# First mixer block of a two-block transformer: stick-breaking heads in two buffers, another order of sums, scores and values, masks in one group, output by row tile

## The chip, the cores and the metric

One NeuronCore of a Trainium2 chip runs the whole kernel. The metric is the time of one execution on the device in microseconds (us), as the median of several runs. TensorE (PE in the profile) multiplies into PSUM, which has eight banks of 512 fp32 columns; VectorE (DVE), ScalarE (ACT) and GpSimd (POOL) work beside it, SyncE (SP) issues the loads of weights. Every engine goes through its own queue in order and waits on semaphores for the others.

## The reference, cut to what matters

Two transformer blocks on 512 tokens of width 1024, all in float32. The change lies in the first block's mixer, where `h` is the normed input times one wide matrix, cut into ten parts:

```
z = (q @ k.T) * scale                         # stick-breaking, 8 heads of 64
log_fail = where(past, log_sigmoid(z) - z, 0)
w = where(past, exp(log_sigmoid(z) + sum of log_fail between), 0)
o_sb = w @ v
log_a = log_sigmoid(g_low @ w_gate_up + b) / 16      # gated linear attention (GLA), 4 heads
o_gla = rms_norm(scan over tokens of decayed k, v, read by q) * silu(g_out)
mix = sigmoid(gate_sb) * (o_sb @ w_proj_sb) + sigmoid(gate_gla) * (o_gla @ w_proj_gla)
x = x + mix @ w_out
```

Then come an MLP of width 4096, a differential attention, an MLP, a short convolution and an MLP, which the change does not touch.

## The kernel before, in words

**Products.** fp32 operands are split into a high and a low part, and a product is three matmuls: high by high, high by low, low by high. Weights are loaded in *quads* of 128x2048 (1 MB) into two slots; ScalarE rounds a quad to `w_hi` (`split_quad`, L1479), VectorE subtracts to `w_lo` (L2017). A slot is free again when TensorE is through with its quad (`quad_done`).

**Woven pieces.** While the attention of the first block runs, the projections that it doesn't need at once (`g_qk`, `g_v`, `gate_sb`, `proj_sb`, `g_out`, `gate_gla`) are woven in: `feed(k)` issues k *pieces*, each 12 matmuls of 512 columns (L881) into one of banks 0 to 3. Four pieces use up one quad. When both quads of a group of four banks are done, VectorE moves each bank out (`move`), and the next group's piece waits for that (`bank_free`).

**A head** of the stick-breaking attention has a chain over all engines. `sb_scores` (L909, with the mask of the diagonal tiles added by a 128x128 matmul, L910) makes the triangle `z` in banks 4 to 6. `sb_soft` on ScalarE takes |z|, exp and log (L1485, L1487, L1489) into the buffer `sb_sp`; VectorE makes the softplus and two tile sums (L2021, L2025, L2027), POOL two more and copies (L569, L572); ScalarE rounds to `sb_hi` (L1499); VectorE subtracts to `sb_lo` (L2031). `sb_sums` (L918, L921) adds the sums of later tokens to `z`; ScalarE takes the exponential twice (L1493, L1494), VectorE subtracts (L2035), `sb_values` (L936) multiplies by the values into bank 7, and VectorE copies a head's output out (L2040). There is one set of the buffers `sb_sp` and `sb_lo`, so `sb_soft` of a head waits for the values of the one before. TensorE's order for head t is written out by hand:

```
for t in range(SB_HEADS):
    if t: feed(4)
    sb_sums(t); feed(2); sb_values(t)
    if t < SB_HEADS - 1: sb_scores(t + 1)
```

The orders of ScalarE, VectorE and POOL are written out in the same way. Before the first head, TensorE turns 31 rows of gains (L960), waits for VectorE to copy them out, and makes the low-rank gate (`gate_low` L946, `gate_up` L956).

**Levels.** GLA is built in eight steps: `level(n)` (L985, 16 matmuls of 128 columns), four pieces behind each of the first seven. POOL makes the differences of the gate sums (`level_diff`, L583, L584), ScalarE their exponentials (`level_exp`, L1516), VectorE the factors (L2134, L2135) and the masked selection (`level_select`, L2142). The first pieces behind level 0 multiply the output of the heads, which ScalarE rounds (L1542) and VectorE subtracts (L2163), 2048 columns each. After the last level the decayed keys (L2198) are turned by TensorE (L1028), then come the states (L991) and the outputs of four row tiles (`gla_out`, L1002, L1004).

**Output of GLA.** Per row tile: VectorE moves it out (L2225), ScalarE squares it (L1576), VectorE and ScalarE make 1/sqrt with a logarithm, an exponential and one Newton step (L1584, L1585, L2230 to L2235), VectorE scales (L2238). TensorE turns the tile (`gla_turn`, L1016), ScalarE writes the high part (L1601), VectorE the low part (L2258), and `multiply_half` (L740) begins `proj_gla`, which goes on at L714.

## Time and profile before

| | |
|---|---|
| median of 3 runs | 2108.38 us (2104.95 to 2108.79) |
| profiled execution: time, span | 2110.67 us, 2108.5 us |
| PE busy | 2023.1 us, 96% of the span |
| DVE, ACT, POOL busy | 1038.4 us (49%), 727.9 us (35%), 144.8 us (7%) |
| granted TensorE clock, mean | 0.986 |
| chain that ended last | PE 83%, DVE 8%, ACT 4%, POOL 2%, issue 2% |
| costliest line | L714 PE, 50% of the chain |

The span is the time from the first to the last instruction of the profiled execution; 2.2 us of its time lie around it. Busy shares are means over stages. The granted clock is the share of full speed at which TensorE may run in a stretch: 1.00 is 2.4 GHz, 0.50 is 1.2 GHz, and values between are stretches with some of both.

### The profile page before, as it was taken

The page shows a single profiled execution, that of the slowest core. Times are in us where ns is not written, and L with a number is a line of the kernel's source. Part 1 is how long each engine was busy: PE and PEld are TensorE (multiplying, and loading weights), DVE is VectorE, ACT ScalarE, POOL GpSimd, SP SyncE. Part 2 cuts the span into 40 slices and gives each one's busy share as a digit, 9 for nine tenths or more (in the row PEclk, how much of TensorE's full clock was granted, in tenths as well). Part 3 has the DMA queues.
Part 4 walks back from the last instruction along what each step waited for, and adds up shares of the span by engine and source line. Part 5 has one row for each costly group of instructions (what it writes and reads, how often), then busy time and mean ns, then how long its engine had stood idle before and what let it go on. Part 6 is the DMA issues. An engine that isn't in the chain of part 4 may idle for free.

```text
span 2108.5 us, 23455 instructions
## 1 busy us (share of the span) xinstructions
PE 2023.1 (96%) x10061; PEld 1702.8 (81%) x10061; DVE 1038.4 (49%) x957; ACT 727.9 (35%) x778; POOL 144.8 (7%) x195
## 2 busy tenths in 40 slices
PE   6998998998999999999999799999999999999998
PEld 5776777877888888888888688888888888888886
DVE  3336457755443334355786653433363646332434
ACT  3343454325232322244455431322331324232222
POOL 1000014000000000011000210000020011000000
PEclk9999999999999999999999999999999999999999
DMA  5311211213232222224222133222323323223231
GB/s 177 100 41 56 64 60 60 80 54 106 90 120 98 86 95 99 100 80 101 65 85 63 60 120 100 87 93 99 100 80 100 100 100 110 88 94 100 99 100 60
DMA packets 98007, 188.44 MB, mean 89 GB/s; under 512 B 3983, under 2 KB 16289, under 8 KB 97921
## 3 DMA queue, kind: packets, MB, share of 16 engines
q1 hardware_dynamic: 93888, 176.17, 25.2%
q0 software_dynamic: 3744, 10.21, 1.8%
q8 instruction: 69, 1.13, 0.2%
q10 hardware_dynamic: 288, 0.79, 0.1%
q14 instruction: 18, 0.14, 0.0%
HBM read 184.01 MB, written 2.10 MB: 88 GB/s over the span
## 4 chain that ended last, share of the span: by engine, by line
PE 83%; DVE 8%; ACT 4%; issue 2%; POOL 2%; DMA 1%; SPq 0%; POOLq 0%; ACTq 0%; DVEq 0%
PE ps L714 50%; PE ps L881 8%; PE ps L726 5%; PE ps L684 4%; PE ps L751 3%; PE ps L1117 2%; PE ps L1123 1%; PE ps L985 1%; PE ps L740 1%; PE ps L1142 1%; PE ps L1071 1%; ACT arena L1639 1%; PE ps L1266 1%; DVE w_lo L1780 1%; DVE w_lo L2017 1%
## 5 line engine op out<-in xcount | busy, mean ns | idle before, releaser
L1780 DVE TENSOR_TENSOR w_lo<-w_raw,w_hi 128x2048 fp32r<-128x2048 f32 x126 | 288.8, 2292 | 714.7 <-ACT w_hi L1318 714.7
L1318 ACT ACTIVATE w_hi<-w_raw 128x2048 fp32r<-128x2048 f32 x126 | 241.5, 1916 | 821.0 <-PE ps L714 684.7
L714 PE MATMUL ps<-a_hi,w_hi 128*128 128x512 f32 x928 | 361.1, 389 | 0.0
L714 PE MATMUL ps<-a_lo,w_hi 128*128 128x512 f32 x928 | 361.1, 389 | 0.0
L714 PE MATMUL ps<-a_hi,w_lo 128*128 128x512 f32 x928 | 361.0, 389 | 0.0
L714 PE MATMUL ps<-w_hi,h_hi 128*128 128x512 f32 x592 | 230.4, 389 | 0.7 <-DVE h_lo L1824 0.7
L714 PE MATMUL ps<-w_hi,h_lo 128*128 128x512 f32 x592 | 230.3, 389 | 0.0
L714 PE MATMUL ps<-w_lo,h_hi 128*128 128x512 f32 x592 | 230.3, 389 | 0.0
L714 PEld LDWEIGHTS ps<-a_hi,w_lo 128*128 128x128 f32 x928 | 174.2, 188 | 36.2
L714 PEld LDWEIGHTS ps<-a_lo,w_hi 128*128 128x128 f32 x928 | 174.2, 188 | 36.1
L714 PEld LDWEIGHTS ps<-a_hi,w_hi 128*128 128x128 f32 x928 | 174.2, 188 | 35.9
L714 PEld LDWEIGHTS ps<-w_hi,h_hi 128*128 128x128 f32 x592 | 111.1, 188 | 24.2 <-issue 1.1
L714 PEld LDWEIGHTS ps<-w_lo,h_hi 128*128 128x128 f32 x592 | 111.1, 188 | 23.1
L714 PEld LDWEIGHTS ps<-w_hi,h_lo 128*128 128x128 f32 x592 | 111.1, 188 | 23.0
L2017 DVE TENSOR_TENSOR w_lo<-w_raw,w_hi 128x2048 fp32r<-128x2048 f32 x36 | 84.0, 2334 | 47.8 <-ACT w_hi L1479 47.7
L535 POOL TENSOR_SCALAR small<-small 128x1 f32<-128x1 f32 x44 | 29.7, 675 | 1125.2 <-ACT qk L1382 1125.2
L1479 ACT ACTIVATE w_hi<-w_raw 128x2048 fp32r<-128x2048 f32 x36 | 68.8, 1912 | 92.1 <-PE ps L881 92.1
L881 PE MATMUL ps<-a_hi,w_hi 128*128 128x512 f32 x192 | 78.6, 410 | 0.0
L881 PE MATMUL ps<-a_lo,w_hi 128*128 128x512 f32 x192 | 76.5, 398 | 0.0
L881 PE MATMUL ps<-a_hi,w_lo 128*128 128x512 f32 x192 | 76.2, 397 | 0.0
L1351 ACT ACTIVATE h_hi<-arena 128x1024 fp32r<-128x1024 f32 x52 | 55.2, 1061 | 53.7 <-DVE arena L1856 40.0
L684 PE MATMUL ps<-w_hi,h_hi 128*128 128x512 f32 x160 | 63.0, 394 | 0.0
(344 smaller groups left out, 3338.0 us busy)
## 6 DMA issues: line engine op xcount, KB each, us to landing
w_raw<-in_w_ff SPq DMA_DIRECT2D x32, 1024.0 KB, 5.1
w_raw<-in_mlp_w_up SPq DMA_DIRECT2D x32, 1024.0 KB, 5.3
w_raw<-in_mlp_w_down SPq DMA_DIRECT2D x32, 1024.0 KB, 5.1
w_raw<-in_w_in SPq DMA_DIRECT2D x26, 1024.0 KB, 5.1
w_raw<-in_attn_w_qkv SPq DMA_DIRECT2D x12, 1024.0 KB, 5.1
w_raw<-in_conv_w_in SPq DMA_DIRECT2D x12, 1024.0 KB, 5.2
w_raw<-in_w_proj_gla SPq DMA_DIRECT2D x4, 1024.0 KB, 5.1
w_raw<-in_w_out SPq DMA_DIRECT2D x4, 1024.0 KB, 5.1
```

The source lines that it names most:

```text
L535: pstep(nc.gpsimd.tensor_scalar(v, sumsq[n % 2][:, i:i + 1], EPS, None, ALU.add))
L684: last = mm(ps[:, bank0 + j], left, right, start=(k == 0 and x == 0), stop=(k == KT - 1 and x == 2))
L714: last = mm(ps[:, bank0 + j], left, right, start=(k == 0 and x == 0), stop=(k == QUAD * quads - 1 and x == 2), skip_group_check=halves)
L726: last = mm(ps[:, bank0 + j], left, right, start=False, stop=(a == QUAD - 1 and x == 2))
L751: last = mm(ps[:, bank0 + j, ts_], left[:, s, a, P * j:P * (j + 1)], right[:, QUAD * qi + a, ts_], start=(half == 0 and qi == 0 and a == 0 ...
L881: last = mm(ps[:, j], left, right, start=(k == 0 and x == 0), stop=(k == QUAD * quads - 1 and x == 2))
L1117: last = mm(ps[:, bank], left[:, k, fs], right[:, k], start=(k == 0 and x == 0), stop=(k == KT - 1 and x == 2))
L1318: nc.scalar.activation(w_hi[:, s], w_raw[:, s], ACT.Copy).then_inc(hi_ready, 1)
L1351: nc.scalar.activation(dst, src, ACT.Copy).then_inc(chunk_hi, 1)
L1479: nc.scalar.activation(w_hi[:, s], w_raw[:, s], ACT.Copy).then_inc(hi_ready, 1)
L1780: tt(w_lo[:, s], w_raw[:, s], w_hi[:, s].bitcast(F32), ALU.subtract).then_inc(lo_ready, 1)
L2017: tt(w_lo[:, s], w_raw[:, s], w_hi[:, s].bitcast(F32), ALU.subtract).then_inc(lo_ready, 1)
```

## The change

It touches the first mixer block alone, in these parts.

- **Start.** The turning of the gains moves ahead, between the two quads of `sb_v`.
- **Heads.** `sb_sp` and `sb_lo` get a second place, in memory of `y_tm`, used by heads 2, 4 and 6; head 0 and the odd heads keep the first. `sb_soft` of a head waits for the values two heads before (head 1 still for those of head 0); the rounding, whose target is shared, still waits for the values one head before. `feed(1)` and the scores of the next head now stand between sums and values.
- **Masks.** The four mask matmuls of a head come after its twelve score matmuls, in one group.
- **Gate.** The log-sigmoid of the gate is one VectorE pass instead of three; its division by 16 goes into the scale of the exponentials. Its scratch lies in `x_tm`.
- **Output of the heads.** Rounded and subtracted in four parts, each with a count of its own; POOL's `level_diff(1)` waits for the last of them.
- **End of the levels.** The decays of keys and queries go ahead of the split of quad 26, on ScalarE and VectorE.
- **Output of GLA.** 1/sqrt is a power on POOL (`refine_gla`), for which ScalarE's squares carry the factor 1/256. `proj_gla` begins with passes that need only the high parts, and the last tiles are turned between the passes. `gla_out(2)` and `gla_out(3)` go one piece earlier. POOL's reload of `x` comes after the four powers.

```diff
@@ -193,7 +193,7 @@
-        u_gate, u_abs, keep = yf[:, 0:2048], yf[:, 2048:4096], yf[:, 2048:4096]
+        u_gate, u_abs, keep = yf[:, 0:2048], xf[:, 0:2048], xf[:, 0:2048]
...
@@ -202,8 +202,12 @@
-        sb_sp, sb_lo, sb_hi = h_hi_f[:, 2048:4096], hhf[:, 2048:4096], hhf[:, 0:2048]
-        sb_t, sb_w, sb_wlo, sb_whi = sb_sp[:, 0:TRI], sb_sp[:, 0:TRI], sb_lo[:, 0:TRI], sb_hi[:, 0:TRI]
+        sb_own = [t % 2 == 1 or t == 0 for t in range(SB_HEADS)]
+        sb_sp = [h_hi_f[:, 2048:4096] if own else yf[:, 2048:4096] for own in sb_own]
+        sb_lo = [hhf[:, 2048:4096] if own else y_r[:, 2048:4096] for own in sb_own]
+        sb_t, sb_w, sb_wlo = ([z_[:, 0:TRI] for z_ in v] for v in (sb_sp, sb_sp, sb_lo))
+        sb_hi = hhf[:, 0:2048]
+        sb_whi = sb_hi[:, 0:TRI]
...
@@ -575,6 +579,8 @@
+                if n == 1:
+                    pool.wait_ge(osb_lo, TT)
...
@@ -591,7 +597,14 @@
+            def refine_gla(c):
+                cs = slice(4 * c, 4 * c + 4)
+                pool.wait_ge(gss_ready, c + 1)
+                pstep(nc.gpsimd.tensor_scalar(gvar[:, cs], gss[:, cs], EPS, None, ALU.add))
+                nc.gpsimd.tensor_tensor(grstd[:, cs], gvar[:, cs], halves, ALU.pow).then_inc(ggs_ready, 1)
+            for c in range(TT):
+                refine_gla(c)
...
@@ -851,7 +864,18 @@
-            gemm("sb_v", A, True)
+            p = ph["sb_v"]
+            for qi in range(2):
+                pe.wait_ge(lo_ready, p.q + qi + 1)
+                if qi == 0:
+                    pe.wait_ge(banks_free, p.b - 1)
+                multiply(hi=a_hi, lo=a_lo, s=slot_of(p, 0, qi), qi=qi, bank0=4 * (p.b % 2), quads=2,
+                         token_major=True).then_inc(quad_done, 1)
+                if qi == 0:
+                    pe.wait_ge(banks_free, p.b)
+                    pe.wait_ge(gains_in, GAIN_LOADS * 16)
+                    nc.tensor.transpose(ps[:, SIDE, 0:N_GAINS], gain_rows[0:N_GAINS],
+                                        ident[0:N_GAINS, 0:N_GAINS]).then_inc(gains_turned, 1)
...
@@ -873,6 +895,8 @@
+                    if name == "proj_sb" and blk == 0 and j == 0:
+                        pe.wait_ge(osb_lo, k + 1)
...
@@ -907,13 +931,14 @@
-                    last = mm(out_[:, 0:P], ident_b[:], strict_b[:], start=False, stop=True, skip_group_check=True)
+                for j in range(TT):
+                    last = mm(z[:, COL[j]:COL[j] + P], ident_b[:], strict_b[:], start=False, stop=True, skip_group_check=True)
...
-                for part in (sb_hi, sb_lo):
+                for part in (sb_hi, sb_lo[t]):
...
@@ -967,10 +990,11 @@
-                feed(2)
-                sb_values(t)
+                feed(1)
...
+                feed(1)
+                sb_values(t)
...
@@ -1037,23 +1061,31 @@
-            feed(2)
+            feed(1)
...
-            feed(3)
+            feed(4)
...
-            for i in range(TT - 1):
-                gla_turn(i)
+            s0, bank0 = slot_of(p, 0, 0), 4 * (p.b % 2)
+            gla_turn(0)
+            gla_turn(1)
...
+            pe.wait_ge(hi_ready, p.q + 1)
+            pe.wait_ge(turned_hi, turn_base["o_gla"] + 4)
+            half_pass(s0, 0, bank0, 0, 0)
+            gla_turn(2)
+            pe.wait_ge(turned_lo, turn_base["o_gla"] + 4)
+            half_pass(s0, 0, bank0, 0, 1)
+            gla_turn(3)
...
-            pe.wait_ge(turned_lo, turn_base["o_gla"] + 4)
-            multiply_half(a_hi, a_lo, slot_of(p, 0, 0), 4 * (p.b % 2), 0, range(0, 2))
-            gla_turn(TT - 1)
-            multiply_half(a_hi, a_lo, slot_of(p, 0, 0), 4 * (p.b % 2), 0, range(2, 4))
+            half_pass(s0, 0, bank0, 0, 2)
+            pe.wait_ge(turned_hi, turn_base["o_gla"] + 8)
+            half_pass(s0, 0, bank0, 1, 0)
...
-            multiply_half(a_hi, a_lo, slot_of(p, 0, 0), 4 * (p.b % 2), 1).then_inc(quad_done, 1)
+            half_pass(s0, 0, bank0, 1, 1)
+            half_pass(s0, 0, bank0, 1, 2).then_inc(quad_done, 1)
...
-            multiply(a_hi, a_lo, slot_of(p, 0, 1), 1, 4 * (p.b % 2), 2, False, True).then_inc(quad_done, 1)
+            multiply(a_hi, a_lo, slot_of(p, 0, 1), 1, bank0, 2, False, True).then_inc(quad_done, 1)
...
@@ -1480,23 +1512,28 @@
             def sb_soft(t):
                 act.wait_ge(z_ready, t + 1)
-                if t:
+                if t and sb_own[t] == sb_own[t - 1]:
                     act.wait_ge(sb_pv, t)
-                nc.scalar.activation(sb_t, z, ACT.Abs).then_inc(sb_abs, 1)
+                elif t:
+                    act.wait_ge(sb_pv, t - 1)
...
@@ -1480,23 +1512,28 @@
-                nc.scalar.activation(sb_hi, sb_sp, ACT.Copy).then_inc(sp_hi, 1)
+                if t:
+                    act.wait_ge(sb_pv, t)
+                nc.scalar.activation(sb_hi, sb_sp[t], ACT.Copy).then_inc(sp_hi, 1)
...
@@ -1522,30 +1559,31 @@
                 act.wait_ge(up_mm, h + 1)
                 nc.scalar.activation(u_gate[:, SEQ * h:SEQ * (h + 1)], ps[:, SIDE], ACT.Identity,
                                      bias=b_gate[:, h:h + 1]).then_inc(u_out, 1)
...
+            for t in range(SB_HEADS):
                 n = 6 + 3 * (t // 2)
...
+                sb_weights(t)
+                if t == SB_HEADS - 1:
+                    break
+                if t % 2 == 0:
+                    split_quad(n + 2)
+                sb_soft(t + 1)
                 if t % 2:
+                    split_quad(n + 4)
+                sb_round(t + 1)
+                if t % 2 == 0:
                     split_quad(n + 3)
...
+                if t == 0:
+                    nc.scalar.activation(u_abs, u_gate, ACT.Abs).then_inc(u_read, 1)
+                    act.wait_ge(u_read, 1)
+                    step(nc.scalar.activation(u_abs, u_abs, ACT.Exp, scale=-1.0))
+                    nc.scalar.activation(u_abs, u_abs, ACT.Ln, bias=1.0).then_inc(gate_log, 1)
+                if t == SB_HEADS - 2:
+                    gate_tiles(gates_sb, 4)
+            level_exp(0)
+            act.wait_ge(osb_out, SB_HEADS)
+            for k in range(TT):
+                nc.scalar.activation(o_hi[:, k], o_sb[:, k], ACT.Copy).then_inc(osb_hi, 1)
+            split_quad(19)
             gate_tiles(gates_sb, 5)
             for n in range(1, 4):
                 level_exp(n)
...
@@ -1560,10 +1598,11 @@
-            split_quad(26)
...
-            nc.scalar.activation(elast, b_cum.rearrange("p (m n) -> p m n", n=P)[:, :, P - 1], ACT.Exp).then_inc(g_exp, 1)
+            nc.scalar.activation(elast, b_cum.rearrange("p (m n) -> p m n", n=P)[:, :, P - 1], ACT.Exp,
+                                 scale=1.0 / GLA_TAU).then_inc(g_exp, 1)
+            split_quad(26)
...
@@ -1601,6 +1625,17 @@
+            gla_squares(0)
+            gla_squares(1)
+            split_quad(28)
+            gla_squares(2)
+            gla_squares(3)
+            gla_high(0)
+            gla_high(1)
+            split_quad(29)
+            gla_high(2)
+            gla_high(3)
...
@@ -2060,12 +2099,9 @@
-            def gate_parts():
-                dve.wait_ge(u_read, 1)
-                step(ts(u_gate, u_gate, 0.0, None, ALU.min))
+            def gate_sum():
...
-                step(tt(u_gate, u_gate, u_abs, ALU.subtract))
-                step(ts(u_gate, u_gate, 1.0 / GLA_TAU, None, ALU.mult))
+                step(stt(u_gate, u_gate, 0.0, u_abs, ALU.min, ALU.subtract))
...
@@ -2074,56 +2110,63 @@
             def gate_scan():
                 nc.vector.tensor_tensor_scan(b_cum, keep, u_gate, 0.0, ALU.mult, ALU.add).then_inc(b_ready, 1)
                 dve.wait_ge(b_ready, 1)
...
+            sb_softplus(0)
+            dve.wait_ge(low_mm, 1)
+            nc.vector.tensor_copy(low_t, ps[0:GLA_RANK, SIDE]).then_inc(low_out, 1)
+            sb_softplus_lo(0)
             for t in range(0, SB_HEADS, 4):
                 n, g = 6 + 3 * (t // 2), 3 * t // 4
...
+                sb_weights_lo(t)
                 split_quad(n + 2)
...
+                sb_softplus(t + 1)
+                sb_out(t)
                 move(g, 0)
                 move(g, 1)
...
+                sb_softplus_lo(t + 1)
                 move(g, 2)
...
                 move(g, 3)
...
                 split_quad(n + 3)
                 sb_weights_lo(t + 1)
+                if t == 0:
+                    gate_sum()
+                sb_softplus(t + 2)
+                sb_out(t + 1)
+                move(g + 1, 0)
                 split_quad(n + 4)
...
+                sb_softplus_lo(t + 2)
+                move(g + 1, 1)
+                move(g + 1, 2)
                 if t == 0:
                     gate_keep()
...
+                move(g + 1, 3)
+                sb_weights_lo(t + 2)
+                split_quad(n + 5)
+                sb_softplus(t + 3)
+                sb_out(t + 2)
+                sb_softplus_lo(t + 3)
+                if t == 0:
                     gate_scan()
...
+                else:
+                    dve.wait_ge(sb_pv, SB_HEADS - 1)
+                    step(nc.vector.memset(g_at, 0.0))
+                split_quad(n + 6)
                 move(g + 2, 0)
                 move(g + 2, 1)
...
+                sb_weights_lo(t + 3)
                 move(g + 2, 2)
...
+                if t + 4 < SB_HEADS:
+                    sb_softplus(t + 4)
+                    sb_out(t + 3)
+                    move(g + 2, 3)
+                    split_quad(n + 7)
+                    sb_softplus_lo(t + 4)
+                else:
+                    move(g + 2, 3)
+                    sb_out(t + 3)
...
             b_chunk = b_cum.rearrange("p (m n) -> p m n", n=P)
...
@@ -2158,9 +2201,10 @@
+            for k in range(TT):
+                dve.wait_ge(osb_hi, k + 1)
+                tt(o_lo[:, k], o_sb[:, k], o_hi[:, k].bitcast(F32), ALU.subtract).then_inc(osb_lo, 1)
...
-            dve.wait_ge(osb_hi, 1)
-            tt(o_lo, o_sb, o_hi.bitcast(F32), ALU.subtract).then_inc(osb_lo, 1)
...
@@ -2193,10 +2237,10 @@
-            split_quad(26)
...
+            split_quad(26)
```

**Order on TensorE around a head's scores.** Before (head 2; ahead of these rows are two pieces and the values' first matmuls):

```order
L936 MATMUL ps<-h_hi,arena_r 128x256 x3
L936 MATMUL ps<-h_hi,arena_r 128x128 x3
L909 MATMUL ps<-qk_r 128x512 [waits w_exp]
L909 MATMUL ps<-qk_r 128x512 x2
L910 MATMUL ps<-strict_b,ident_b 128x128
L909 MATMUL ps<-qk_r 128x384 x3
L910 MATMUL ps<-strict_b,ident_b 128x128
L909 MATMUL ps<-qk_r 128x128 x3
L910 MATMUL ps<-strict_b,ident_b 128x128
L909 MATMUL ps<-qk_r 128x256 x3
L910 MATMUL ps<-strict_b,ident_b 128x128
L881 MATMUL ps<-a_hi,w_hi 128x512 [waits lo_ready]
```

With the change (head 3; pieces, L905, on both sides, the values, L961, one piece later):

```order
L905 MATMUL ps<-w_hi,a_hi 128x512
L905 MATMUL ps<-w_lo,a_hi 128x512
L905 MATMUL ps<-w_hi,a_lo 128x512
L933 MATMUL ps<-qk_r 128x512 [waits w_exp]
L933 MATMUL ps<-qk_r 128x512 x2
L933 MATMUL ps<-qk_r 128x384 x3
L933 MATMUL ps<-qk_r 128x128 x3
L933 MATMUL ps<-qk_r 128x256 x3
L935 MATMUL ps<-strict_b,ident_b 128x128 x4
L905 MATMUL ps<-w_hi,a_hi 128x512 [waits bank_free]
L905 MATMUL ps<-w_lo,a_hi 128x512
L905 MATMUL ps<-w_hi,a_lo 128x512
```

The scores no longer follow the values, pieces stand on both sides of them, and the masks come together at their end.

**Order on ScalarE in two heads.** Before (weights of head 3, a split, softplus and rounding of head 4, a split, its weights):

```order
L1493 ACTIVATE h_hi_f<-ps 128x1280 [waits c_ready]
L1494 ACTIVATE h_hi<-ps 128x1280
L1479 ACTIVATE w_hi<-w_raw 128x2048 [waits quad_done,raw_full1]
L1485 ACTIVATE h_hi_f<-ps 128x1280 [waits sb_pv,z_ready]
L1487 ACTIVATE h_hi_f<-h_hi_f 128x1280 [waits sb_abs]
L1489 ACTIVATE h_hi_f<-h_hi_f 128x1280 [waits sb_exp]
L1499 ACTIVATE h_hi<-h_hi_f 128x2048 [waits sp_after,sp_summed]
L1479 ACTIVATE w_hi<-w_raw 128x2048 [waits quad_done,raw_full0]
L1493 ACTIVATE h_hi_f<-ps 128x1280 [waits c_ready]
```

With the change (weights of head 2 in the second buffer, split, softplus and rounding of head 3 in the first, split, its weights):

```order
L1528 ACTIVATE y_tm<-ps 128x1280 [waits c_ready]
L1529 ACTIVATE h_hi<-ps 128x1280
L1511 ACTIVATE w_hi<-w_raw 128x2048 [waits quad_done,raw_full1]
L1520 ACTIVATE h_hi_f<-ps 128x1280 [waits sb_pv,z_ready]
L1522 ACTIVATE h_hi_f<-h_hi_f 128x1280 [waits sb_abs]
L1524 ACTIVATE h_hi_f<-h_hi_f 128x1280 [waits sb_exp]
L1536 ACTIVATE h_hi<-h_hi_f 128x2048 [waits sb_pv,sp_after,sp_summed]
L1511 ACTIVATE w_hi<-w_raw 128x2048 [waits quad_done,raw_full0]
L1528 ACTIVATE h_hi_f<-ps 128x1280 [waits c_ready]
L1529 ACTIVATE h_hi<-ps 128x1280
```

The softplus of the next head still follows the weights, with a split between; its scores come before the values now, and the target alternates between `h_hi_f` and `y_tm`.

**Order on VectorE at the end of the levels.** Before (silu, split of quad 26, decayed keys and queries, last selection):

```order
L2155 TENSOR_TENSOR arena<-arena 128x4x512 [waits gates_made]
L2017 TENSOR_TENSOR w_lo<-w_raw,w_hi 128x2048 [waits hi_ready]
L2198 TENSOR_TENSOR h_lo_f<-h_lo_f,qk 128x2048 [waits g_exp]
L2199 TENSOR_TENSOR h_lo_f<-h_lo_f,h_hi_f 128x2048
L2142 COPY_PREDICATED y_tm<-masks,ps 128x2048 [waits g_sel,g_mm,dve_step]
```

With the change:

```order
L2198 TENSOR_TENSOR arena<-arena 128x4x512 [waits gates_made]
L2241 TENSOR_TENSOR h_lo_f<-h_lo_f,qk 128x2048 [waits g_exp]
L2242 TENSOR_TENSOR h_lo_f<-h_lo_f,h_hi_f 128x2048
L2056 TENSOR_TENSOR w_lo<-w_raw,w_hi 128x2048 [waits hi_ready,dve_step]
L2185 COPY_PREDICATED y_tm<-masks,ps 128x2048 [waits g_sel,g_mm]
```

The split, which waits for TensorE to finish a quad, has moved behind the two decays.

## Rows read from the trace of the kernel before

**Rows 1.** Waits of TensorE up to 500 us: total us, times, longest us.
```profile
PE ps L918 <- DVE h_hi L2031: 6.3, 6, 4.0
PE ps L1016 <- DVE a_lo L2258: 6.0, 1, 6.0
PE ps L881 <- issue: 5.7, 1, 5.7
PE ps L1028 <- DVE y_tm L2142: 3.7, 1, 3.7
PE ps L946 <- DVE gains L2008: 3.2, 1, 3.2
PE ps L936 <- DVE h_hi L2035: 2.2, 1, 2.2
```

**Rows 2.** Stretches (from:to, length, busy us and instructions by engine, PEclk, DMA share, GB/s).
```profile
99.39:105.50 6.11, 6.11 (x14) 4.79 (x15) 2.35 (x4) 2.72 (x2) 1.33 (x4) 0.50 0.34 130
136.30:139.50 3.20, 3.20 (x10) 2.52 (x10) 0.00 (x0) 2.83 (x3) 0.00 (x0) 0.50 0.00 0
176.70:180.00 3.30, 3.29 (x13) 3.00 (x13) 3.30 (x1) 0.00 (x0) 0.00 (x0) 0.58 0.00 0
265.70:269.00 3.30, 3.30 (x11) 2.58 (x11) 0.10 (x1) 3.02 (x3) 0.00 (x0) 0.54 0.86 259
323.70:327.50 3.80, 3.72 (x9) 2.98 (x10) 3.80 (x1) 3.59 (x2) 3.80 (x2) 0.51 0.00 0
436.10:440.00 3.90, 3.82 (x16) 3.50 (x17) 2.54 (x3) 0.00 (x0) 0.00 (x0) 0.57 0.00 0
491.50:495.00 3.50, 3.41 (x17) 3.44 (x18) 2.92 (x8) 1.68 (x4) 0.00 (x0) 0.54 0.77 292
```

**Rows 3.** Stretches: one level with four pieces behind it; the four pieces alone.
```profile
336.47:350.94 14.47, 14.47 (x81) 12.58 (x80) 10.85 (x8) 1.91 (x1) 4.38 (x2) 1.00 0.22 72
339.96:350.94 10.98, 10.98 (x51) 9.10 (x50) 8.87 (x7) 0.00 (x0) 4.38 (x2) 1.00 0.30 96
```

**Rows 4.** Timeline of one head (start us, us, engine, line, out<-in [idle before <-releaser]).
```profile
190.39 0.68 DVE L2040 COPY arena<-ps 64x512 f32<-64x512 f32 x1 [2.21 <-PE ps L936]
...
193.66 1.24 ACT L1485 ACTIVATE h_hi_f<-ps 128x1280 f32<-128x1280 f32 x1 [11.10 <-PE ps L910]
...
197.55 1.49 DVE L2021 SCALAR_TENSOR_TENSOR h_hi_f<-ps,h_hi_f 128x1280 f32<-128x1280 f32 x1 [6.48 <-ACT h_hi_f L1489]
...
200.56 1.92 ACT L1499 ACTIVATE h_hi<-h_hi_f 128x2048 fp32r<-128x2048 f32 x1 [3.04 <-POOL h_hi_f L572]
...
202.51 2.29 DVE L2031 TENSOR_TENSOR h_hi<-h_hi_f,h_hi 128x2048 fp32r<-128x2048 f32 x1 [2.67 <-ACT h_hi L1499]
...
204.85 0.85 PE L918 MATMUL ps<-h_hi,ntri 128*128 128x512 f32 x3 [0.26 <-DVE h_hi L2031]
...
207.08 1.24 ACT L1493 ACTIVATE h_hi_f<-ps 128x1280 f32<-128x1280 f32 x1 [2.80 <-PE ps L921]
```

**Rows 5.** Timeline, TensorE: masks in the scores here and in the later attention.
```profile
191.17 0.23 PE L910 MATMUL ps<-strict_b,ident_b 128*128 128x128 bf16 x1
...
191.33 0.79 PE L909 MATMUL ps<-qk_r 64*128 64x384 f32 x3
...
1029.70 0.40 PE L1178 MATMUL ps<-causal_b,ident_b 128*128 128x128 bf16 x4
```

**Rows 6.** Timeline, ScalarE: the third level exponential.
```profile
331.47 1.92 ACT L1516 ACTIVATE h_hi_f<-h_hi_f 128x2048 f32<-128x2048 f32 x1 [4.10 <-POOL h_hi_f L584]
```

**Rows 7.** Timeline, VectorE, ahead of the transposed keys.
```profile
425.47 2.29 DVE L2017 TENSOR_TENSOR w_lo<-w_raw,w_hi 128x2048 fp32r<-128x2048 f32 x1 [4.15 <-ACT w_hi L1479]
```

**Rows 8.** Timeline, TensorE and ScalarE, where the output is turned.
```profile
483.83 1.80 PE L1016 MATMUL ps<-consts,arena 128*128 128x128 f32 x15
...
486.88 3.01 ACT L1601 ACTIVATE a_hi<-ps,gains 128x256 fp32r<-128x256 f32 x8
```

**Rows 9.** Groups by form, POOL: a small power (busy us, mean ns, idle us).
```profile
L536 POOL TENSOR_TENSOR small<-small 128x1 f32<-128x1 f32 x44 | 39.3, 893 | 3.7
```

141 lines of the change are left out of this document (38 added, 103 removed).

## The prediction

> **What bounds the kernel now.** I read the page first: TensorE is busy for 96% of the span and holds 83% of the chain that ended last. So only what TensorE waits for, what its own instructions take and which clock it is granted can move the time. A busier or idler VectorE costs nothing until TensorE waits for it. The waits of TensorE come next: ahead of 500 us, outside the first 95 us, six groups stand for 27.1 us [rows 1]. The reader is to see that all of them lie in the block that is changed, and that only two are made of several pieces. Third, the table of stretches. After each of the long waits, and twice without one (at 136.3 and 265.7), TensorE runs for 3 to 6 us at half clock or near it [rows 2]. A stretch of length L with granted clock c gives back L x (1 - c): 3.1 + 1.6 + 1.4 + 1.5 + 1.9 + 1.7 + 1.6 = 12.8 us. The block's own work is dense elsewhere: a level with four pieces takes 14.47 us, the four pieces 10.98, one piece 2.74 [rows 3].
>
> **Start.** The turning of the gains moves into `sb_v`, where VectorE waits between two splits, so their copy is over before the scores end. Its 3.2 us of wait (L946) go [rows 1], and with them the 6.1 us at half clock behind it, 3.1 us [rows 2]. Gain 6.3.
>
> **Heads.** From the last mask to the sums, the chain takes 11.2 us: softplus on ScalarE from 193.66, VectorE from 197.55, rounding from 200.56, subtraction 202.51 to 204.80, sums at 204.85 [rows 4]. TensorE has four pieces, 10.98, as cover [rows 3], so a usual head waits only 0.26. In two heads VectorE was late with gate work, and those hold most of the 6.3 of L918 and all the 2.2 of L936 [rows 1]. With the change the scores stand one piece and the values earlier, so five pieces and the values cover the chain: 13.7 us and more against 11.2. The rounding still waits for the values of the head before, and from there only 1.9 + 2.3 lie ahead of the sums. VectorE also has two passes less over the gate. So all 8.5 us go, and the low clock at 136.3, 176.7 and 265.7, 4.5 us. For the two without a wait ahead I note that values and scores stood together just before; a piece now parts them.
>
> Two new waits come in. Head 1 still uses head 0's buffer, so its softplus starts only at the end of values 0. VectorE's queue has that softplus ahead of the output's copy and of bank 0's, which the ninth piece needs: 3.9 + about 2.3 + 0.7 + 0.7 = 7.6 us after the values [rows 4] (the copies from L2040, a like size), against two pieces, 5.5. TensorE waits 2.1. After that, ScalarE has rounding, a split and three passes over the gate to do ahead of head 1's weights: 3.9 + 3.0 + 1.9 + 1.9 + 5.8 and two exponentials of 1.2 are 18.9 us after values 0, where TensorE wants scores 2 after 5.5 + 2.1 + 5.5 + 2.2 + 2.7 = 18.0. Wait 0.9. In all other heads scores wait for those two exponentials, which begin at 207.08 [rows 4] and end 2.4 later, under one piece of 2.74; the margin is 0.3, so I charge nothing. Heads: 8.5 + 4.5 - 3.0 = 10.0.
>
> **Masks.** A mask between scores takes 0.16 from its start to the next start; four in a row in the later attention take 0.40 with the last one's whole length of 0.23, so 0.06 each [rows 5]. Three of the four masks of a head, and perhaps the last, save 0.10: 8 x 0.33 = 2.6 us at most; bounds 0 and 2.6, and I take 2.6, since L1178 is the same instruction with the same kinds of operands.
>
> The Trainium skill ("TensorE: Matmul & The Clock Gate", LDWEIGHTS) puts a load of 128 columns at 128/1.2, some 107 ns, whatever it holds. By it a mask in a group would stay at 0.11, and the masks would give an estimated 1.7. The rows disagree: 0.06 from start to start.
>
> **Output of the heads.** The wait of 5.7 before the first piece of `proj_sb` (L881) [rows 1] is for one rounding and one subtraction of 2048 columns, after each other. In four parts of about 0.5 and 0.6 the last is ready 3.1 us after level 0 began, and level 0 takes 3.5 (14.47 less 10.98) [rows 3]. Wait gone, and 1.9 of low clock at 323.7. But POOL's differences now begin at that end, 3.9 later than before. The third exponential began at 331.47 [rows 6], 17.2 after level 0; now 21.1. Behind it come 1.9, a split 1.9 on ScalarE, 2.3 on VectorE and a selection, which I take at 2.5 for its 2048 columns: 29.7, where level 2 wants to start at 28.9. New wait 0.8. Gain 5.7 + 1.9 - 0.8 = 6.8.
>
> **End of the levels.** VectorE idled 4.15 ahead of the split of quad 26 [rows 7], with the two decays (2.3 each) behind it. Now they lie in that gap, and the last selection ends 4.5 earlier. The 3.7 of L1028 go, and 1.7 of low clock: 5.4.
>
> **Output of GLA.** TensorE turned three tiles only after VectorE's low parts: 6.0, L1016 [rows 1]. Now it needs the high parts of two tiles: turning takes 1.8, ScalarE's eight copies 3.0 from half a microsecond after the start [rows 8], so a wait of 1.8 stays. Then the passes cover the rest: 16 matmuls of 256 columns take 2.0, a turning 0.9, and the ScalarE split between takes 1.9. The powers on POOL take 0.9 for one column [rows 9]; even at twice that they end before VectorE comes to them, and two outputs go a piece earlier. The reload of `x` on POOL's queue starts somewhat later and is not needed before `w_out`. Gain 6.0 - 1.8 = 4.2, and 1.6 of low clock at 491.5 if it doesn't return: 5.8.
>
> **Sum.** 6.3 + 10.0 + 2.6 + 6.8 + 5.4 + 5.8 = 36.9 us. The clock is what I trust least. Waits of 1.8 to 2.2 remain, one of them next to turning. In the trace 2.2 at L936 was followed by no low stretch, but two stretches came with no wait at all. I leave two stretches of 1.6 in place: 33.7. Against the profiled execution's 2110.7 that is 2077.0; it ran 2.3 above the median of 2108.4, so 2074.7 for the median.
>
> The Trainium skill (same page, Part 4) says that transposes don't count as activity for the clock. By it turning and wait together, 1.8 + 1.8, would look idle and the output of GLA would keep its 1.6. That it happens there or elsewhere, the two stretches left in the sum hold it.
>
> **Rivals.**
> *The clock isn't given back* (18%). Waits go, but low stretches stay as long as before at other places; 136.3 and 265.7 speak for it, the missing one after L936 against. 36.9 - 12.8 = 24.1, so 2084.3.
> *VectorE's queue makes the new wait* (10%). What I charge in head 1 alone happens in all seven: softplus ahead of the bank copies. For it: ScalarE's softplus comes behind a split in half of the heads. Against: in the later heads softplus starts with the scores, one piece and the values earlier, which leaves over 2 us. At 2.1 each in six more heads, 12.6 less: 2087.3.
> *Masks cost the same in a group, buffers buy nothing* (7%). The change doesn't do what it says there: a usual head waited 0.26 only, so two buffers alone are worth about 1.3. 33.7 - 2.6 - 1.3: 2078.6.
> *Slower: TensorE at half clock in the heads* (3%). Half-row scores, short sums and values are now scattered between pieces; if each head drew low stretches, each of 3.2 us would cost 1.6. To eat 36.9 us and 4.2 more, it takes 26, over three in each head; from there on the kernel is slower, about 2113. The trace has two in seven heads without a wait.
>
> **How the numbers follow.** My forecast has 62%: 2074.7, its own range 2069 to 2081. The range reaches down to 2067 (all of 36.9, a full set of masks and the lower edge of the runs, 3.4 under the median) and up to 2088, which takes in the first three rivals. A measurement here tells about 0.2%, 4.2 us, from no change. Faster by more: 0.96; within: 0.01; slower: 0.03.
>
> **What would show it.** TensorE's waits up to 475 us under 8 us, and none for the gains, for VectorE's subtraction at the first head-output piece, or at the transposed keys. A wait near 2 in head 1 for VectorE's bank copy, one below 1 ahead of scores 2, one near 1.8 between turning and the first pass. Mask rows of x4 with 0.40. Usual heads closer together by 0.6 (0.26 and the masks' 0.33). It is wrong if sums still wait in later heads, if level 1 or 2 wait more than 1 us for the selection, or if the stretches at half clock add up to more than 6 us of loss in the block.

## The result, and the profile after

The changed kernel takes 2067.66 us (median of four runs, 2065.21 to 2069.64) against 2108.59 for the kernel before (2104.95 to 2108.84): 40.9 us less. The ratio on record is 0.9817, 95% interval 0.9805 to 0.9829; the two medians by themselves give 0.9806. The forecast was 2074.7 with 2067 to 2088, so the time lies in the range, but only 0.7 us above its lower end, and below the forecast's own 2069 to 2081. The profiled execution of the changed kernel took 2065.21 us, its span is 2063.4, its mean granted clock 0.996 (before 0.986).

TensorE's waits up to 500 us in the changed kernel (total, times, longest). They answer to [rows 1]; L784 lies in the work ahead of the block and waited 19.0 before as well.

```profile
PE ps L784 <- DVE y_tm L1920: 19.0, 3, 14.0
PE ps L905 <- DVE h_lo_f L2088: 2.1, 1, 2.1
PE ps L764 <- ACT a_hi L1625: 1.9, 1, 1.9
PE ps L905 <- DVE qk L2096: 1.6, 1, 1.6
PE ps L1009 <- DVE arena L2079: 0.9, 1, 0.9
PE ps L933 <- ACT h_hi L1529: 0.6, 1, 0.6
```

Sums (L943) and values (L961) are gone from the list, and so are the gains and the transposed keys. What the block still waits is 7.1 us, against 28.0 before: 27.1 of [rows 1] and a wait of 0.9 at L985 that was there too and stayed (L1009).

The whole block, from the first scores to the first product of `proj_gla` at full width (busy us and instructions by engine, granted clock, DMA share, GB/s): before, then after with one usual head.

```profile
92.60:506.30 413.70, 385.68 (x1886) 318.97 (x1886) 243.87 (x228) 180.21 (x162) 46.11 (x47) 0.96 0.20 64
```
```profile
92.80:464.90 372.10, 364.97 (x1886) 308.07 (x1886) 235.56 (x207) 177.78 (x157) 53.48 (x55) 1.00 0.22 71
190.00:212.80 22.80, 22.80 (x115) 19.05 (x113) 11.70 (x12) 9.88 (x7) 1.33 (x4) 1.00 0.28 93
```

The block is 41.6 us shorter, and the granted clock in it is 1.00: none of the seven low stretches of [rows 2] is left. Of the 41.6, 20.9 are waits (28.0 less 7.1) and 12.8 the low stretches; that leaves 7.9, and most of it is in scores and masks. These are the rows of head 4's scores in the changed kernel, beside [rows 5]:

```profile
192.88 2.19 PE L933 MATMUL ps<-qk_r 64*128 64x512 f32 x12
195.01 0.40 PE L935 MATMUL ps<-strict_b,ident_b 128*128 128x128 bf16 x4
195.21 0.48 PE L905 MATMUL ps<-w_hi,a_hi 128*128 128x512 f32 x1
```

From the first score to the piece behind the masks it is 195.21 - 192.88 = 2.33 us. Before, the same stretch (of head 3) is this:

```profile
190.28 0.96 PE L909 MATMUL ps<-qk_r 64*128 64x512 f32 x3
...
193.40 0.23 PE L910 MATMUL ps<-strict_b,ident_b 128*128 128x128 bf16 x1
193.44 0.48 PE L881 MATMUL ps<-w_hi,a_hi 128*128 128x512 f32 x1
```

That is 3.16 us. Each of eight heads saves 0.83, 6.6 us in all; I had forecast 0.33 and 2.6. Two usual heads are now 22.79 us apart (scores at 170.09 and 192.88) instead of 24.08 (190.28 and 214.36), 1.29 less: 0.83 for the masks, 0.26 for the wait, and 0.20 that I can't place, which over seven heads is about the rest of the 7.9. The chain of the same head, which answers to [rows 4], now ends in time:

```profile
195.44 1.24 ACT L1520 ACTIVATE y_tm<-ps 128x1280 f32<-128x1280 f32 x1 [2.92 <-PE ps L935]
...
202.31 1.92 ACT L1536 ACTIVATE h_hi<-y_tm 128x2048 fp32r<-128x2048 f32 x1 [1.22 <-POOL y_tm L576]
...
205.17 2.29 DVE L2070 TENSOR_TENSOR y_r<-y_tm,h_hi 128x2048 fp32r<-128x2048 f32 x1
...
210.85 0.73 PE L943 MATMUL ps<-h_hi,ntri 128*128 128x512 f32 x3
```

The subtraction ends at 207.46 and the sums start at 210.85 without a wait, a margin of 3.4 us. The program behind the block, which the change does not touch, is 3.7 us shorter in this execution (from 506.3 and 464.9 to the end). Nearly all of it is the clock. In the kernel before, two waits of TensorE there, of 1.8 and 2.5 us, were each followed by a stretch at half clock, 3.4 us in all:

```profile
979.40:982.80 3.40, 3.40 (x10) 2.62 (x9) 1.74 (x4) 2.03 (x3) 0.00 (x0) 0.50 0.00 0
1136.40:1139.80 3.40, 3.40 (x9) 2.63 (x9) 2.88 (x9) 0.23 (x2) 0.00 (x0) 0.50 0.72 278
```

In the changed kernel the same two waits (1.5 and 2.5) were not. Of the twelve profiles below five have neither stretch. So these come and go from one execution to the next; without them the spans differ by 41.7, near the 40.9 between the medians.

### The profile page after: what moved, and what is told of

Same layout as the page of the kernel before. It is cut to its first block, busy times and chain, and to the rows that moved or that the text cites. A ratio compares the mean times of both kernels' runs of the same rounds, so it can differ in the third digit from the quotient of the medians.

```text
span 2063.4 us, 23442 instructions
## 1 busy us (share of the span) xinstructions
PE 1999.3 (97%) x10061; PEld 1689.5 (82%) x10061; DVE 1030.2 (50%) x938; ACT 726.2 (35%) x773; POOL 152.9 (7%) x203
## 4 chain that ended last, share of the span: by engine, by line
PE 87%; DVE 6%; ACT 3%; POOL 1%; DMA 1%; issue 1%; SPq 0%; POOLq 0%; ACTq 0%; DVEq 0%
PE ps L727 51%; PE ps L905 11%; PE ps L739 5%; PE ps L697 4%; PE ps L764 4%; PE ps L1149 2%; PE ps L1155 1%; PE ps L1009 1%; PE ps L1103 1%; PE ps L933 1%; PE ps L1174 1%; ACT arena L1674 1%; PE ps L1298 1%; DVE w_lo L2056 1%; PE ps L961 1%
## 5 line engine op out<-in xcount | busy, mean ns | idle before, releaser
L905 PE MATMUL ps<-a_hi,w_hi 128*128 128x512 f32 x192 | 77.2, 402 | 2.1 <-DVE h_lo_f L2088 2.1
L905 PE MATMUL ps<-a_hi,w_lo 128*128 128x512 f32 x192 | 74.9, 390 | 0.0
L905 PE MATMUL ps<-a_lo,w_hi 128*128 128x512 f32 x192 | 74.8, 390 | 0.0
```

The source lines that it names most:

```text
L905: last = mm(ps[:, j], left, right, start=(k == 0 and x == 0), stop=(k == QUAD * quads - 1 and x == 2))
```

## The experiments

Twelve kernels. "Against" is the difference of medians to the kernel named; the ratio is to the kernel before, run beside it on the same chip. The median of the kernel before was 2108.59 beside the changed kernel and 2106.01 to 2107.41 beside the others, so a difference to the changed kernel can be off by some 2.6 us. The last column leaves that out: it is the same difference in the profiled executions, for the block alone, from head 0's first score to the first product of `proj_gla` at full width (413.7 us before, 372.1 in the changed kernel).

| | median us | ratio to before (95%) | against | block in the trace |
|---|---|---|---|---|
| masks only | 2098.19 | 0.9958 (0.9945 to 0.9972) | before -9.2 | -8.1 |
| half-row masks | 2098.98 | 0.9963 (0.9951 to 0.9974) | before -8.4 | -8.3 |
| start only | 2100.10 | 0.9966 (0.9954 to 0.9978) | before -7.3 | -7.4 |
| masks apart | 2079.14 | 0.9859 (0.9840 to 0.9878) | changed +11.5 | +12.9 |
| old order, two buffers | 2081.20 | 0.9883 (0.9868 to 0.9898) | changed +13.5 | +14.3 |
| new order, one buffer | 2082.23 | 0.9889 (0.9874 to 0.9905) | changed +14.6 | +15.9 |
| head output whole | 2068.58 | 0.9818 (0.9804 to 0.9831) | changed +0.9 | +1.7 |
| and factor ahead of it | 2073.13 | 0.9843 (0.9829 to 0.9857) | changed +5.5 | +6.6 |
| split 26 first | 2075.01 | 0.9844 (0.9829 to 0.9859) | changed +7.4 | +8.4 |
| low parts first | 2068.56 | 0.9817 (0.9802 to 0.9832) | changed +0.9 | +0.2 |
| waits taken out | 2062.11 | 0.9788 (0.9775 to 0.9802) | changed -5.6 | -5.3 |
| select ahead of split | 2059.55 | 0.9779 (0.9764 to 0.9793) | changed -8.1 | -6.7 |

### What the masks cost

Masks alone, in the kernel before:

```diff
-                    last = mm(out_[:, 0:P], ident_b[:], strict_b[:], start=False, ...)
+                for j in range(TT):
+                    last = mm(z[:, COL[j]:COL[j] + P], ident_b[:], strict_b[:], start=False, ...)
```

> The kernel before with the four masks of a head behind its twelve score matmuls, and nothing else. Theory A (a switch between 64-row score matmuls and 128-row masks leaves a load of weights uncovered, about 0.1 us each time): scores and masks of a head take 2.3 instead of 3.3 us, 0.8 to 1.0 less in each of 8 heads, gain 6.6 to 8 us. Theory B (the prediction's: only the mask itself is shorter, 0.06 instead of 0.16): 0.33 a head, gain 2.6 us. The low stretches at 136 and 266 us stay under both; if they go, the masks between the scores drew them, and the gain has 3.1 us more.

The same line the other way round, in the changed kernel:

> The changed kernel with each mask back behind its three score matmuls. Theory A (row switches): 0.8 to 1.0 us more in each head, slower than the changed kernel by 6.6 to 8 us, about 2075. Theory B (mask alone): slower by 2.6 us, about 2070. If masks between scores draw low clock, stretches at half clock come back behind scores and it is slower by 3 us more.

And the masks left in place in the kernel before, over 64 rows (half of each mask is then left out of the result):

```diff
-                    last = mm(out_[:, 0:P], ident_b[:], strict_b[:], ...)
+                    last = mm(out_[:, 0:P], ident_b[rows], strict_b[rows], ...)
```

> The kernel before with each mask left in its place but made over the 64 rows that the head's scores use, not over 128; half of each mask is left out of the result. Theory A (what costs is the switch between 64 and 128 rows): a head's scores and masks fall from 3.3 to about 2.4 us although the masks stand between, gain about 6 us. Theory C (what costs is the switch between fp32r and bf16 operands): they stay at 3.3, gain 0. Theory B (mask alone): a mask stays at 0.16, gain 0.

Theory B falls in all three, C in the third. TensorE's timeline with half-row masks, head 4:

```profile
209.55 0.96 PE L909 MATMUL ps<-qk_r 64*128 64x512 f32 x3
210.36 0.23 PE L910 MATMUL ps<-strict_b,ident_b 64*128 64x128 bf16 x1
210.40 0.76 PE L909 MATMUL ps<-qk_r 64*128 64x384 f32 x3
...
212.05 0.50 PE L881 MATMUL ps<-w_hi,a_hi 128*128 128x512 f32 x1
```

The masks are still bf16 between fp32r matmuls, yet the next score starts 0.04 us behind a mask, not 0.16, and the mask starts 0.81 behind its first score, not 0.89 [rows 5]. The stretch takes 2.50 instead of 3.16. Before, the array went between 128 and 64 rows eight times in a head (once from the values, seven times around masks); here, and with the masks in a group, twice. Six switches fewer for 0.66 us: 0.11 each on the average. The Trainium skill ("TensorEngine Tiling (Array Packing)", Key Properties) says that changing the tiling mode drains TensorE. The trace agrees in so far as each change costs, 0.11 us here; what TensorE does in that time it does not show. Grouping the masks adds the 0.17 that is left of the 0.83, close to half of the prediction's 0.33.

Direct savings are then 8 x 0.83 = 6.6 and 8 x 0.66 = 5.3 us, but 9.2 and 8.4 were measured, and 8.1 and 8.3 in the block of the traces. The rest goes with the clock: in neither profile is there a low stretch without a wait ahead of it, where the kernel before has two, at 136.3 and 265.7 [rows 2], 3.1 us together. It doesn't add up to the tenth, since the waits move as well (29.7 us in the block with grouped masks, 28.1 with half-row masks, 28.0 before). In the changed kernel with masks apart they come back, behind scores and with TensorE busy all through (columns as in [rows 2]):

```profile
125.40:128.80 3.40, 3.40 (x10) 2.72 (x10) 0.63 (x1) 0.00 (x0) 0.00 (x0) 0.51 0.44 107
152.60:159.40 6.80, 6.80 (x20) 5.28 (x21) 2.11 (x2) 3.78 (x3) 0.00 (x0) 0.51 0.00 0
203.90:207.30 3.40, 3.40 (x11) 2.67 (x10) 0.00 (x0) 2.95 (x3) 0.00 (x0) 0.51 0.02 5
```

These cost 13.6 x 0.49 = 6.7 us, and 6.6 + 6.7 is 13.3, where the block is 12.9 longer. The four runs spread from 2073.6 to 2081.2, granted clock 0.994 to 0.991: the fastest is 6.0 above the changed kernel's median, with a clock that the changed kernel's runs have too (0.993 to 0.996), so it carries the masks' direct cost and hardly a low stretch more. Masks apart do not bring the low clock each time. The profiles with masks apart have two (before), three (here) and none (start only) of these stretches without a wait; the eleven with grouped or half-row masks have none in this block. That speaks for masks apart as a condition, but it is a count over few executions. The scatter goes the same way: the three kernels with masks apart spread over 7.8, 7.6 and 6.6 us, the other eleven over 0.8 to 5.8, the changed kernel over 4.4.

### Start

The kernel before with the part "Start" of the change alone, on TensorE and VectorE.

> The kernel before with the turning of the gains inside sb_v, and nothing else. Theory A (the low stretch at 99 us hangs on the wait of 3.2 us ahead of it): wait and stretch go, gain 6.3 us. Theory B (the clock falls there for another reason, the work of the start): only the wait goes, gain 3.2 us, and a stretch of about 6 us at 0.50 stays near 96 us.

Theory A: 7.3 us (7.4 in the block of the trace), no wait at `gate_low`, and a granted clock of 1.00 up to 170 us. That last is why it is more than 6.3: the stretch at 136.3, which has no wait ahead of it, is missing as well, 1.6 us, though the masks still stand apart; the sums wait 0.7 more (7.0 against 6.3). Instead of the stretch at 265.7 there is one at 272.6, behind a wait of 1.8 at the sums.

### Heads: order and buffers

```diff
-                feed(1)
-                if t < SB_HEADS - 1:
-                    sb_scores(t + 1)
-                feed(1)
+                feed(2)
                 sb_values(t)
+                if t < SB_HEADS - 1:
+                    sb_scores(t + 1)
```

> The changed kernel with TensorE's old order in the heads (sums, two pieces, values, scores), everything else as changed, two buffers too. Theory A (what the order buys is cover for the chain from scores to sums): four pieces of 10.98 stand against a chain of 11.2, 0.26 a head, slower than the changed kernel by about 1.8 us, 2069.5; masks stay in one group, so no low stretch comes where values and scores adjoin. Theory B (with the new order of VectorE, softplus ahead of the bank copies, a late softplus makes bank copies late as in head 1): 2.1 us in four to six heads besides, slower by 10 to 14 us, about 2080. If values and scores side by side draw low clock by themselves, stretches at half clock come back behind them, 1.7 us each.

```diff
-        sb_own = [t % 2 == 1 or t == 0 for t in range(SB_HEADS)]
+        sb_own = [True] * SB_HEADS
```

> The changed kernel with one pair of buffers for all heads, TensorE's new order kept. Each softplus waits for the values of the head before, as that of head 1 does in the changed kernel. Theory A (the buffers only give the chain its cover): 0.26 in each of seven heads, 1.8 us slower, 2069.5. Theory B (head 1's wait of 2.1 for VectorE's bank copy comes in the heads whose copies stand behind a softplus): four to six times 2.1 and 1.8, slower by 10 to 14 us, 2078 to 2082. Either way waits of 2 us may be followed by half clock, 1.7 us each; without such stretches the two figures hold.

The sizes are theory B's, the places are not. TensorE's waits with the old order and two buffers:

```profile
PE ps L943 <- DVE y_r L2069: 6.6, 3, 3.8
PE ps L961 <- DVE h_hi L2073: 2.8, 2, 1.6
PE ps L905 <- DVE h_lo_f L2087: 2.0, 1, 2.0
PE ps L905 <- DVE x_tm L2089: 2.0, 1, 2.0
...
PE ps L943 <- DVE h_hi L2069: 0.5, 2, 0.2
```

Bank copies wait twice only (heads 1 and 5). Most of it is at sums and values. For head 2, VectorE shows why:

```profile
160.74 2.28 DVE L2055 TENSOR_TENSOR w_lo<-w_raw,w_hi 128x2048 fp32r<-128x2048 f32 x1
162.93 2.29 DVE L2069 TENSOR_TENSOR y_r<-y_tm,h_hi 128x2048 fp32r<-128x2048 f32 x1
```

A split of weights stands ahead of the subtraction that the sums wait for (at 165.27, after 1.64). In the changed kernel the same split stands in the same place, and its margin covers it (3.4 us in the head shown above). The waits are 13.9 us against 2.7 in the heads of the changed kernel, 11.2 more, and a stretch at half clock comes behind the wait of 3.8. One buffer gives nearly the same list (7.5, 2.1, 2.1, 1.2). So order and buffers are not two gains to be added: without either, the whole of some 14 us is lost. That is more than the 10.0 of the prediction's term. I take it that the new orders of ScalarE and VectorE rely on both; they were not tried apart.

### Output of the heads

Whole again (one rounding, one subtraction, no wait on POOL), and then also VectorE's factor of level 0 ahead of the subtraction:

```diff
-            for k in range(TT):
-                dve.wait_ge(osb_hi, k + 1)
-                tt(o_lo[:, k], o_sb[:, k], ...).then_inc(osb_lo, 1)
+            dve.wait_ge(osb_hi, 1)
+            tt(o_lo, o_sb, ...).then_inc(osb_lo, 1)
             level_factor(0)
```

> The changed kernel with the output of the heads rounded and subtracted in one instruction each again, and the wait of the level differences on it taken out, as before. Theory A (the whole part is worth what the prediction says): wait of 5.7 at the first piece of proj_sb and a low stretch behind it come back, 7.6 us, and the wait of 1.6 behind level 1 (bank copy of VectorE) goes, since the differences begin earlier: slower by 6.0 us, about 2073.7. Theory B (the low clock at 324 hung on masks and scores, not on the wait): only 5.7 less 1.6, slower by 4.1 us, 2071.8.

```diff
+            level_factor(0)
             dve.wait_ge(osb_hi, 1)
             tt(o_lo, o_sb, ...).then_inc(osb_lo, 1)
-            level_factor(0)
```

> The version with the whole output of the heads, and VectorE's factor of level 0 back ahead of the subtraction, the order before. Theory A (most of the old wait of 5.7 was the two products of the factor, 5.1 us, standing ahead of the subtraction in VectorE's queue): the wait goes from 1.4 back to about 5.7 and half clock follows it: slower than that version by 4.3 and 1.9 less what level 2's wait of 1.6 gives back, 2073 to 2075. Theory B (one rounding and one subtraction by themselves made it): no change, 2068.6.

Both theories of the first fall: 0.9 us between the medians, 1.7 in the block. Its waits at this place:

```profile
PE ps L1007 <- DVE y_tm L2182: 1.6, 1, 1.6
PE ps L903 <- DVE arena_r L2202: 1.4, 1, 1.4
```

The whole output costs a wait of 1.4, and the 1.6 move from the bank copy to the selection ahead of level 1 (L1007 at 307.73 is level 1; the second expectation calls it level 2's wait). With the factor ahead it is the old figure:

```profile
PE ps L903 <- DVE arena_r L2203: 5.7, 1, 5.7
```

It is 4.6 us slower than whole output alone, as expected (4.3 and 1.9 less 1.6); in the block of the traces 4.9, with 1.7 in it from a low stretch in head 1 (136.4 to 139.8) that has nothing to do with this place. VectorE in the kernel before:

```profile
314.19 2.30 DVE L2134 TENSOR_TENSOR qk<-qk,h_lo_f 128x1024 f32<-128x1024 f32 x1
316.41 2.91 DVE L2135 TENSOR_TENSOR qk<-qk,h_lo_f 128x1024 f32<-128x1024 f32 x1
319.24 4.44 DVE L2163 TENSOR_TENSOR arena_r<-arena,arena_r 128x2048 fp32r<-128x2048 f32 x1
```

The rounding was done at 316.11. The subtraction waited 3.1 us more for two products of the level, and then took 4.44 where the same shape takes 2.29 elsewhere (a split, [rows 7]), while POOL was making differences. In the changed kernel POOL waits for the subtraction, and four parts take 2.50 together. The split in four is the smallest share of this term: without it a wait of 1.4 comes back, of 5.7.

### End of the levels

The changed kernel with `split_quad(26)` ahead of the decays again, on both engines.

> The changed kernel with the split of quad 26 ahead of the two decays again, on ScalarE and VectorE. Theory A (the prediction's term): wait of 3.7 at the transposed keys and a low stretch of 3.9 us behind it come back, slower by 5.4 us, 2073.1. Theory B (no low stretch without masks apart): slower by 3.7 us, 2071.4.

The wait is there, 3.7 us, with half clock behind it, and one stretch more:

```profile
405.40:411.00 5.60, 5.60 (x20) 4.93 (x21) 2.77 (x3) 0.00 (x0) 0.00 (x0) 0.50 0.00 0
```
```profile
458.80:462.20 3.40, 3.40 (x21) 3.40 (x19) 2.39 (x2) 1.38 (x3) 0.00 (x0) 0.56 0.00 0
```

Theory A holds in kind: wait and stretch come back. In size it is 7.4 us between the medians, not 5.4, and 8.4 in the block: 3.7 of wait, 2.8 for the first stretch, which is longer than the 3.9 us before, and 1.5 for the second. Two of five runs are at 2072.4 and 2072.6, 4.7 and 5.0 above the changed kernel; the others, the profiled one among them (2076.9), took longer. The second stretch stands behind turning and its wait of 1.9, the place of the Trainium skill's rule that transposes don't count ("TensorE: Matmul & The Clock Gate", Part 4). In the one-buffer kernel there is such a stretch too (465.7 to 469.3, 0.53); in the changed kernel and four of its other variants with the same wait there is none. Two of seven profiles: no run here shows whether turning or the wait draws it.

### Output of GLA

TensorE's old order at the end (three tiles turned, products with high and low parts from the start), everything else as changed.

> The changed kernel with TensorE's old order at the output of GLA: three tiles turned, then products that need high and low parts from the start. The powers on POOL stay. Theory A (the order of turning and passes is the whole of this part's gain): the wait goes from 1.9 to 6.0 and half clock follows it, slower by 4.1 and 1.6, 2073.4. Theory B (the earlier powers and outputs carry a share): the wait comes back to 4 or 5 only, slower by 2 to 4 us, 2070 to 2072.

Neither theory: 0.9 us, inside the scatter, and 0.2 in the block. The waits are 1.4 and 0.5, together the 1.9 of the changed kernel:

```profile
PE ps L1040 <- DVE a_lo L2277: 1.4, 1, 1.4
...
PE ps L753 <- DVE a_lo L2277: 0.5, 1, 0.5
```

What had made 6.0 is on the other queues. Before, turning began at 483.83 [rows 8] and ScalarE and VectorE had this to do first:

```profile
485.08 1.89 ACT L1479 ACTIVATE w_hi<-w_raw 128x2048 fp32r<-128x2048 f32 x1
486.88 3.01 ACT L1601 ACTIVATE a_hi<-ps,gains 128x256 fp32r<-128x256 f32 x8
```
```profile
486.00 1.67 DVE L2238 SCALAR_TENSOR_TENSOR arena<-y_tm,small,arena 128x256 f32<-128x256 f32 x4
487.59 2.28 DVE L2017 TENSOR_TENSOR w_lo<-w_raw,w_hi 128x2048 fp32r<-128x2048 f32 x1
489.79 3.22 DVE L2258 SCALAR_TENSOR_TENSOR a_lo<-ps,gains,a_hi 128x256 fp32r<-128x256 f32 x8
```

The high parts started 3.0 us and the low parts 6.0 us behind the turning, after the split of quad 29 and the late scale of tile 3. In the changed kernel, where that split comes later in both queues, it is 0.6 and 1.5 (TensorE, ScalarE, VectorE). No run puts the split back by itself, so its share is read from these rows and not tested against that of the powers on POOL and the earlier outputs:

```profile
447.74 1.91 PE L1040 MATMUL ps<-consts,arena 128*128 128x128 f32 x16
```
```profile
448.38 3.02 ACT L1625 ACTIVATE a_hi<-ps,gains 128x256 fp32r<-128x256 f32 x8 [8.29 <-PE ps L1040]
```
```profile
449.25 3.23 DVE L2284 SCALAR_TENSOR_TENSOR a_lo<-ps,gains,a_hi 128x256 fp32r<-128x256 f32 x8 [0.62 <-ACT a_hi L1625]
```

### The waits that were left

Five edits to the changed kernel, one for each wait, and a sixth in the last kernel. The core of them:

```diff
@@ VectorE, head 0 @@
-                sb_softplus(t + 1); sb_out(t); move(g, 0); move(g, 1)
+                move(g, 0); move(g, 1); sb_out(t); sb_softplus(t + 1)
@@ VectorE, levels @@
-            level_factor(1); moves(6)
+            moves(6); level_factor(1)
@@ ScalarE, three passes over the gate @@
-                if t == 0:
+                if t == 1:
@@ TensorE, level 0: wait for osb_out moved @@
+                    if n == 0 and m == 12:
+                        pe.wait_ge(osb_out, SB_HEADS)
@@ TensorE, first pass (tiles 0 and 1 turned half by half) @@
-            pe.wait_ge(turned_hi, turn_base["o_gla"] + 4)
+            pe.wait_ge(turned_hi, turn_base["o_gla"] + 2)
@@ VectorE, last kernel only @@
-            split_quad(20); level_select(1)
+            level_select(1); split_quad(20)
```

> The changed kernel with its five remaining waits of TensorE in this block taken on: VectorE copies out the first two banks and head 0's output ahead of the softplus of head 1 (wait 2.1); ScalarE's three passes over the gate stand behind the rounding of head 2 (0.6); VectorE moves the first output banks out ahead of the factor of level 1 (1.6); the last head's output is waited for only by the level's last four products (0.9); tiles 0 and 1 are turned half by half, so that the first pass waits for two halves, not four (1.9 becomes 0.4). Theory A (each wait is a matter of one queue's order): 6.7 us faster than the changed kernel, 2061.0. Theory B (the work in VectorE's queue is late as a whole, the waits only move on): half of it or less, 2064 to 2067.

> The version with the waits taken out, and the selection of level 1 ahead of the split of quad 20 on VectorE. Theory A (the wait of 1.1 ahead of level 2 is that queue order): 1.1 us faster than that version, 2061.0, and the piece behind level 2 doesn't wait for the split. Theory B (the split is then late instead): no change, 2062.1, with a wait of about 1 us at the first piece behind level 2.

The first gains 5.6 of the 6.7: four of the waits are gone and one is 0.4, but 1.1 came up ahead of level 2 and 0.3 at the sums of head 1. With the sixth edit the 1.1 goes as well. TensorE's waits in the whole block of the last kernel:

```profile
PE ps L769 <- ACT a_hi L1638: 0.4, 1, 0.4
PE ps L948 <- DVE h_hi L2082: 0.3, 1, 0.3
```

This is the fastest version, 8.1 us under the changed kernel between the medians and 6.7 in the block. Of the 2.6 between the two, 1.3 show between the starts of levels 1 and 2 in their profiles (300.81 and 316.65, then 300.01 and 314.55); the kernel before ran 1.1 faster beside the second, which is most of the rest.

## Why the prediction was right or wrong

**Start.** Right in kind: 3.2 of wait and 3.1 of clock went, and alone it measured 7.3.

**Heads.** Forecast 10.0; in the trace waits fell from 8.5 to 2.7 and 4.5 of low clock went, 10.3. The new wait for the bank copy in head 1 is 2.1, as forecast, that ahead of scores 2 is 0.6, not 0.9. What the step did not see is that the term exists only with order and buffers together, given the new queues of ScalarE and VectorE: it put 1.3 on the buffers by themselves, and taking them away costs 14.6. Two of the three low stretches in this term (136.3 and 265.7) had no wait ahead of them, and by the runs on masks they go with the masks rather than with the order.

**Masks.** This term was mis-sized: 2.6 forecast, 6.6 measured. The step "three of the four masks of a head, and perhaps the last, save 0.10" priced the mask and took the scores between them as unchanged. The rows to read stood in the trace: a mask of 0.16 to the next start, between rows of 64 partitions. And it had 0 and 2.6 as bounds; 2.6 was no upper bound.

**Clock.** "I leave two stretches of 1.6 in place" was the other miss: none stayed. The two stretches without a wait were put down to values and scores side by side. With the old order and grouped masks those are side by side in seven heads, and the profile has no stretch there but the one behind a wait of 3.8. Half-row masks, with everything else as before, took both away; start only took them away too, with masks apart, so one execution proves little.

**Sum.** The mechanisms were right and the total was 7.2 too small. By the trace the terms are 6.3, 10.3, 6.6, 6.0, 5.4 and 5.7, 40.3 us, 6.6 more than the 33.7: 4.0 for the masks, 3.2 for the two stretches that did not stay, 0.3 for the heads, 0.8 and 0.1 less for the two outputs. The 1.3 that I can't place make it the 41.6 of the block; 40.9 is between medians. The low clock in these terms is that of one execution of the kernel before (clock 0.986, where most of its 15 later runs have 0.987 to 0.989), so the agreement to a microsecond is partly luck. So is the hit: the range reached 2067 by an allowance of 3.4 for the lower edge of the runs, and what filled it was the masks and the clock.

**Output of the heads.** 6.8 forecast, 6.0 in the trace (5.7 and 1.9 less a new 1.6). Right in size, wrong in cause: "one rounding and one subtraction after each other" needed some 4 us, the rest was VectorE's queue and POOL beside it. The new wait was forecast as 0.8 ahead of level 2. It came as 1.6 one step earlier, at the bank copy behind level 1, because that copy stands on VectorE behind two products of level 1, which are slow while POOL works (the same products of level 2 take 1.21 and 1.22):

```profile
302.94 2.75 DVE L2177 TENSOR_TENSOR qk<-qk,h_lo_f 128x1024 f32<-128x1024 f32 x1
305.61 3.14 DVE L2178 TENSOR_TENSOR qk<-qk,h_lo_f 128x1024 f32<-128x1024 f32 x1
308.67 2.47 DVE L2096 TENSOR_TENSOR qk<-ps,qk 128x512 f32<-128x512 f32 x4
...
318.85 1.21 DVE L2177 TENSOR_TENSOR h_hi_f<-h_hi_f,h_lo_f 128x1024 f32<-128x1024 f32 x1
```

With the copies put ahead of the products that wait was gone.

**End of the levels.** 5.4 forecast; 3.7 of wait and 1.7 of clock went. Right.

**Output of GLA.** 5.8 forecast, 5.7 in the trace (6.0 less 1.9, and 1.6). Size right, cause wrong: the passes that need only high parts bring 0.9 us at most. By the rows it is the split of quad 29, now behind the first high and low parts. The step counted ScalarE's copies "from half a microsecond after the start [rows 8]", but those rows have 3.0 (483.83 to 486.88); that the new queue brings it down to 0.6 was assumed, and it carried the term.

**Rivals.** In this block the clock was given back in full, VectorE's queue made its wait in head 1 alone among the heads, masks did not cost the same, and no head drew half clock. The second rival's price, 12.6, is about what either half of the heads' part would have cost by itself.
